# A two-layer diffusion backbone on one NeuronCore: the first adaLN modulation computed with its weights as the stationary operand, group by group

## The reference, cut to what matters

```
mod_x = silu(c) @ w_ada[l] + b_ada[l]          # latent tokens
mod_c = silu(c_ctx) @ w_ada[l] + b_ada[l]      # context tokens
sh1, sc1, g1, sh2, sc2, g2 = split(mod, 6)     # 1024 each
h = rmsnorm(x, g_attn[l]) * (1 + sc1) + sh1    # then h @ w_in[l] and the attention
```

## Time and profile before

| | |
|---|---|
| median of 3 runs | 2082.66 us (2076.31, 2084.02, 2082.66) |
| span of the profiled execution | 2084.2 us |
| PE busy | 1818.6 us, 87% of the span |
| DVE busy | 1218.3 us, 58% |
| ACT busy | 828.5 us, 40% |
| POOL busy | 630.4 us, 30% |
| HBM traffic | 161.48 MB read, 4.19 MB written |

### The profile page before, as it was taken

The page is one execution under the profiler, slowest core; times in us unless marked ns, Lnnn a source line. Parts: engine busy times, 40 slices in busy tenths (PEclk is TensorE's granted clock), DMA queues, the critical chain, the costliest instruction groups (busy, mean ns, idle before and its releaser), DMA issues.

```text
span 2084.2 us, 26369 instructions
## 1 busy us (share of the span) xinstructions
PE 1818.6 (87%) x9456; PEld 1556.0 (75%) x9456; DVE 1218.3 (58%) x2125; ACT 828.5 (40%) x1452; POOL 630.4 (30%) x324
## 2 busy tenths in 40 slices
PE   5877987786896998999999978799886889999997
PEld 1776777674685887888888868778775668888886
DVE  2765757656558688755415665576566466335255
ACT  3345664545423333133213334465555334334242
POOL 1123532212111333422322322252322124444442
PEclk9988999896897999999999989799996889999999
DMA  8210013000142223333324331100100123232332
GB/s 327 85 45 8 1 57 106 20 21 1 61 152 71 99 95 139 123 130 121 101 81 130 122 117 54 38 1 16 51 21 21 51 71 101 93 99 91 101 100 82
DMA packets 45166, 166.94 MB, mean 80 GB/s; under 512 B 4752, under 2 KB 4752, under 8 KB 43920
## 3 DMA queue, kind: packets, MB, share of 16 engines
q1 hardware_dynamic: 41696, 156.25, 22.2%
q10 hardware_dynamic: 3376, 9.44, 1.2%
HBM read 161.48 MB, written 4.19 MB: 79 GB/s over the span
## 4 chain that ended last, share of the span: by engine, by line
PE 67%; DVE 16%; issue 9%; ACT 5%; DMA 2%; DVEq 0%; SPq 0%; POOL 0%; ACTq 0%
PE ps L736 19%; PE ps L737 18%; PE ps L738 18%; DVE nb L1636 2%; PE ps L834 2%; DVE ada_junk L1339 2%; PE ps L835 2%; PE ps L755 2%; PE ps L845 2%; DVE pt_lo L1613 1%; PE ps L933 1%; PE ps L720 1%; ACT qk L1085 1%; DMA w_raw<-w_d 1%; DVE p_sb L1605 1%
## 5 line engine op out<-in xcount | busy, mean ns | idle before, releaser
L667 POOL TENSOR_TENSOR w_lo<-w_raw,w_hi 128x1024 fp32r<-128x1024 f32 (+1 forms) x200 | 474.1, 2374 | 1195.0 <-ACT w_hi L1007 1195.0
L736 PE MATMUL ps<-h_hi,w_hi 128*128 128x512 f32 (+1 forms) x1056 | 376.2, 356 | 5.9 <-DVE h_lo L1427 5.9
L737 PE MATMUL ps<-h_lo,w_hi 128*128 128x512 f32 (+1 forms) x1056 | 376.0, 356 | 0.0
L738 PE MATMUL ps<-h_hi,w_lo 128*128 128x512 f32 (+1 forms) x1056 | 375.2, 355 | 0.0
L1007 ACT ACTIVATE w_hi<-w_raw 128x1024 fp32r<-128x1024 f32 (+1 forms) x200 | 201.3, 1007 | 360.5 <-PE ps L738 236.5
L736 PEld LDWEIGHTS ps<-h_hi,w_hi 128*128 128x128 f32 x1056 | 201.0, 190 | 34.8 <-issue 6.4
L698 POOL TENSOR_TENSOR p_sb<-p_sb,ri 128x768 f32<-128x768 f32 (+1 forms) x120 | 156.1, 1307 | 233.3 <-DVE p_sb L1605 126.6
L737 PEld LDWEIGHTS ps<-h_lo,w_hi 128*128 128x128 f32 x1056 | 201.1, 190 | 28.0
L738 PEld LDWEIGHTS ps<-h_hi,w_lo 128*128 128x128 f32 x1056 | 200.8, 190 | 28.1
L736 PE MATMUL ps<-w_hi,h_hi 128*128 128x384 f32 (+1 forms) x560 | 191.0, 341 | 17.2 <-DVE h_lo L1427 12.4
L1636 DVE TENSOR_REDUCE nb<-ps 128x1 f32<-128x768 f32 (+1 forms) x160 | 135.1, 847 | 111.7 <-PE ps L835 111.4
(11 more groups left out here) (133 smaller groups left out, 3315.4 us busy)
## 6 DMA issues: line engine op xcount, KB each, us to landing
w_raw<-w_d SPq DMA_DIRECT2D x152, 512.0 KB, 3.5
ada_b<-ada_d SPq DMA_DIRECT2D x64, 512.0 KB, 3.6
w_raw<-w_d SPq DMA_DIRECT2D x48, 384.0 KB, 3.1
ada_first<-first_d SPq DMA_DIRECT2D x4, 2048.0 KB, 19.7
ada_first<-ada_d SPq DMA_DIRECT2D x4, 1024.0 KB, 11.5
x_sb<-x_d SPq DMA_DIRECT2D x1, 3072.0 KB, 12.1
x_sb<-x_d ACTq DMA_DIRECT2D x1, 3072.0 KB, 10.3
c_bc<-cc_d SPq DMA_DIRECT2D x2, 1024.0 KB, 8.8
```

The lines of the kernel that those rows point to most:

```text
L667: nc.gpsimd.tensor_tensor(w_lo[:, c % RING, 0:n], w_raw[:, c % RAW, 0:n], w_hi[:, c % RING, 0:n].bitcast(f32), ALU.subtract).then_inc(w_lo ...
L736: nc.tensor.matmul(out, lh, rh, start=first, stop=False)
L737: nc.tensor.matmul(out, lh, rl_, start=False, stop=False)
L738: return nc.tensor.matmul(out, ll, rh, start=False, stop=last)
```

## The change

The stationary and the moving operand change places. For each output feature tile j of a group and each of the eight contraction tiles k, a 128 x 128 block of the weights is the stationary operand and the two columns of silu_cols are the moving one, so that the result stands as feature columns in PSUM at once. `mod_row`, ACT's four copies and PE's sixteen transposes go. The columns of the weights are put in another order in HBM (by the host, as before), so that group g holds scale and shift of the tiles k = 2g and 2g + 1. PE makes groups 0 and 1 ahead of `norm_stats` and groups 2 and 3 behind it. DVE reads groups 0 and 1 before tile k = 0 of the norm, group 2 before k = 2 and group 3 before k = 6. The first projection's matmuls into banks 0 to 3 wait for DVE's read of that group's bank.

```diff
-            def first_modulation():
+            def first_modulation(groups):
-                pe.wait_ge(silu_cols_done, 1)
                 width = FIRST_GROUP * P
-                def columns(g):
-                    pe.wait_ge(mod_row_copied, g + 1)
-                    for c in range(g * FIRST_GROUP, (g + 1) * FIRST_GROUP):
-                        mm = nc.tensor.transpose(ps[:, 4, 2 * c:2 * c + 2], mod_row[:, c * P:(c + 1) * P],
-                                                 ident[0:2, 0:2])
-                    mm.then_inc(first_mod_done, 1)
-                for g in range(FIRST_ADA // FIRST_GROUP):
+                for g in groups:
                     pe.wait_ge(first_ada_loaded[g], 16)
                     w = ada_first[:, g * FIRST_GROUP:(g + 1) * FIRST_GROUP, :].rearrange("p a k -> p (a k)")
-                    for k in range(KT):
-                        mm = nc.tensor.matmul(ps[0:2, g, 0:width], silu_cols[:, k, :],
-                                              w[:, k * width:(k + 1) * width], start=k == 0, stop=k == KT - 1)
-                    mm.then_inc(mod_row_done, 1)
-                    if g:
-                        columns(g - 1)
-                columns(g)
+                    for j in range(FIRST_GROUP):
+                        for k in range(KT):
+                            at0 = k * width + j * P
+                            mm = nc.tensor.matmul(ps[:, g, 2 * j:2 * j + 2], w[:, at0:at0 + P], silu_cols[:, k, :],
+                                                  start=k == 0, stop=k == KT - 1)
+                    mm.then_inc(first_mod_done, 1)
...
                 if l == 0:
+                    pe.wait_ge(silu_cols_done, 1)
+                    first_modulation((0, 1))
                     norm_stats(0)
-                    first_modulation()
+                    first_modulation((2, 3))
...
+                            elif l == 0 and p == 0 and c == 0 and t < FIRST_ADA // FIRST_GROUP:
+                                pe.wait_ge(first_mod_read, t + 1)
...
-                    for g in range(FIRST_ADA // FIRST_GROUP):
-                        act.wait_ge(mod_row_done, g + 1)
-                        width = FIRST_GROUP * P
-                        A(mod_row[:, g * width:(g + 1) * width], ps[0:2, g, 0:width], ACT.Copy) \
-                            .then_inc(mod_row_copied, 1)
...
-            def first_modulation():
-                dve.wait_ge(first_mod_done, FIRST_ADA // FIRST_GROUP)
+            def first_modulation(g):
+                dve.wait_ge(first_mod_done, g + 1)
+                src = ps[:, g, 0:2 * FIRST_GROUP].rearrange("p (k a s) -> p k a s", k=2, a=2)
+                for a, at0 in enumerate((KT + 2 * g, 2 * g)):
+                    for s in range(2):
+                        ins = V.tensor_tensor(mod[:, s, at0:at0 + 2], src[:, :, a, s],
+                                              sm[:, S_BADA + at0:S_BADA + at0 + 2], ALU.add)
+                        if a and s:
+                            ins.then_inc(first_mod_read, 1)
+                        else:
+                            step.mark(ins)
+                step.wait()
+                dve.wait_ge(first_mod_read, g + 1)
                 for s in range(2):
-                    src = ps[:, 4, 0:2 * FIRST_ADA].rearrange("p (c s) -> p c s", s=2)[:, :, s]
-                    step(V.tensor_tensor(mod[:, s, 0:FIRST_ADA], src, sm[:, S_BADA:S_BADA + FIRST_ADA], ALU.add))
-                V.memset(zero[:, :], 0.0).then_inc(ada_used, FIRST_ADA)
-                norm_gains(gs1, KT, S_GATTN)
+                    step.mark(V.scalar_tensor_tensor(gs1[:, s, 2 * g:2 * g + 2], mod[:, s, KT + 2 * g:KT + 2 * g + 2],
+                                                     1.0, sm[:, S_GATTN + 2 * g:S_GATTN + 2 * g + 2],
+                                                     ALU.add, ALU.mult))
+                step.wait()
...
                 if j == 0:
-                    first_modulation()
+                    V.memset(zero[:, :], 0.0).then_inc(ada_used, FIRST_ADA)
...
                 for k in range(KT):
+                    if j == 0:
+                        for g in {0: (0, 1), 2: (2,), 6: (3,)}.get(k, ()):
+                            first_modulation(g)
```

More of the change, by code:

```diff
@@ L330, in backbone @@
     ada_first = place("ada_first", [P, FIRST_ADA, D], f32, R_H)
-    mod_row = place("mod_row", [2, FIRST_ADA * P], f32, R_QKV + 20 * KB)
     ada_b = [place(f"ada_b{i}", [P, D], f32, R_O + (14 + 4 * i) * KB) for i in range(2)]
@@ L413, in backbone @@
         silu_cols_done = sem("silu_cols_done")
-        mod_row_done = sem("mod_row_done")
-        mod_row_copied = sem("mod_row_copied")
+        first_mod_read = sem("first_mod_read")
         first_mod_done = sem("first_mod_done")
@@ L1851 @@
     n_first = FIRST_ADA // FIRST_GROUP
-    first = np.asarray(w_ada)[0][:, :FIRST_ADA * P].reshape(KT, P, n_first, FIRST_GROUP * P)
+    order = [c for k in range(KT) for c in (KT + k, k)]
+    first = np.asarray(w_ada)[0][:, :FIRST_ADA * P].reshape(KT, P, FIRST_ADA, P)[:, :, order, :]
+    first = first.reshape(KT, P, n_first, FIRST_GROUP * P)
     first = np.ascontiguousarray(first.transpose(2, 1, 0, 3).reshape(n_first, P, -1))
```

## The result

The changed kernel takes 2094.28 us (median of 4 runs, 2093.60 to 2096.78) against 2082.39 us (4 runs of before, 2076.31 to 2084.02): ratio 1.0053, interval 1.0037 to 1.0069, so 11.9 us slower by the medians. Run again on another occasion, six runs against eleven, the ratio was 1.0056 (1.0041 to 1.0072).

What follows compares the result with a forecast made beforehand. The first modulation, then DVE's chain to the split at 120.69 us, was taken as the bound. Tile 6 11.4 us later gave 2084.2 + 11.4 = 2095.6 us profiled, 2094.0 us against the median; range 2084 to 2099 us.

Steps and rivals of the forecast that it cites:

- The price of a pass: New modulation's 256 records on PE: 0.213 us each at clock 0.50, 13.65 us for a group.
- Landings and groups: Start of kernel: groups land at 20.7, 25.6, 30.5 and 37.4 us; PE ends group 1 at 48.0 us.
- Statistics: Behind group 1 on PE: 6.45 us as before, to 54.5 us, starting 25.1 us later.
- Rival C: Start of kernel: POOL beside the diagonals and DVE's small readings cost their upper ends, up to +14 us, 2096.5 us; chance 0.07.
- DVE's reading of a group: Before the norm's tiles: four additions and two gains, 1.4 us, bounds 1.0 and 1.8 us.
- DVE's modulation tiles: Behind the norm on DVE's chain to the split: follow by the same 11.4 us.
- Tile 6: Norm on DVE, after waiting for group 3: starts at 83.3 instead of 71.94 us, 11.4 us later.
- PE's wait for the split: In the projection: PE arrives at 128.2 us, split about 132.1 us; wait shrinks from 8.5 to about 4 us.
- The end: Behind 121 us nothing is touched, it only shifts; 2094.0 us against the median.
- Rival A: Modulation: passes raise and hold the clock, 0.112 us each behind 29.46 us; tile 6 10.3 us earlier, 2072.3 us; chance 0.12.
- Rival B: Group 2: spreading of 1/rms lifts the clock for 3.4 us, saving 3.1 us: +8.3 us, 2091.0 us; chance 0.25.

Runs made afterwards that it cites:

- High parts early: Changed kernel with ACT's high parts of units 2 and 3 ahead of the square root, so POOL's splits precede DVE's diagonals: 2093.30 us, ratio 1.0033.
- 128 columns and slow diagonals: Changed kernel with silu_cols repeated to 128 moving columns instead of two, nothing else altered: 2074.21 us, ratio 0.9957.
- quick diagonals: Changed kernel with 128 moving columns and ACT's high parts of units 2 and 3 ahead of the square root: 2067.32 us, ratio 0.9917.

## Why the prediction was right

The forecast was 2094.0 us, the measurement 2094.28 us. By its own steps:

- **The price of a pass**, 0.213 us, which everything hung on: 0.213 and 0.212 us in the changed kernel. That these passes neither raise nor hold the clock was argued from 9.7 us of line 865; the run with all groups behind the statistics shows it over 47.2 us, and 128 moving columns in the same passes undo it.
- **Landings and groups**: group 0 at 20.5 us (forecast 20.7), statistics at 47.84 us (48.0).
- **Statistics**: forecast 6.45 us, measured 8.53 us. This is the term that was mis-sized. I had taken nothing for POOL's splits beside DVE's diagonals, because at 27 us these were paced by PE, with 1.5 us as upper end; they took 4.40 instead of 1.6 us. High parts early took 2.2 us of it back. The measured 2.1 us lies above the upper end of 1.5 us that I had kept. Rival C has an error of its own: its two upper ends, 1.5 us here and 0.4 us for reading group 3, give 13.3 us and not 14 us.
- **DVE's reading of a group**: forecast 1.4 us, measured 84.45 - 83.72 = 0.73 us; four additions pipeline in 0.36 us. That gave back 0.7 us.
- **DVE's modulation tiles**, taken as merely shifted: of the 16 products four take 2.6 us or more, each beside a split of POOL, where three did before, and the last ends 14.8 us late (121.5 instead of 106.7 us).
- **Tile 6**: forecast 83.3 us, measured 84.45 us, so 12.5 instead of 11.4 us late; DVE idle ahead of group 2 for 8.73 (I had said some 11) and ahead of group 3 for 4.40 us (4).
- **PE's wait for the split**: forecast 3.9 us, measured 4.40 us. PE's delay at the start of the projection, 83.54 - 65.84 = 17.7 us, is hidden as far as it exceeds DVE's 13.3 us.
- **The end**: 11.9 us by the medians, less than the 13.3 us at the split. The nearness of the totals to 0.3 us is luck: the statistics were 2.1 us too short and the reading 0.7 us too long, the split came 1.9 us later than forecast, and the part of the shift that is lost behind it hid most of that.

Rival A, the clock raised by the passes, is what 128 columns make of the kernel: forecast for it was tile 6 at 61.6 us and 10.3 us gained; measured 63.31 us, of which 2.8 us are diagonals, and a ratio of 0.9957. The rule that speaks for it in the Trainium skill's page "TensorE: Matmul & The Clock Gate", in "Why this matters for your kernels", that an engine kept busy gets its full clock, did not hold for passes with two moving columns: 0.50 over 47.2 us of gapless records. The same page's section "LDWEIGHTS (loading the stationary operand)" gives a load one price, its columns divided by 1.2 GHz, and no second one for the other level of the clock; here the same load came every 0.11 us at 1.00 and every 0.21 us at 0.50. Rival B occurred in the run with all groups behind the statistics, as a stretch of 3.4 us, and saved there about the 3.1 us that were forecast for it: 256 passes took 51.51 us, where 256 x 0.212 us are 54.3 us. Neither profile of the changed kernel holds a level before 86 us, but the spacing of 0.212 us over groups 2 and 3 leaves no room for it there.

Not settled: why the shift, 13.3 us at the split, is 11.3 us at the feed-forward of layer 0 and 7.5 us at the end of one profile, 9.4 and 8.0 us in the other. Part of it is PE itself. PE busy behind the split, before and then in the changed kernel:

```profile
121.00:2084.00 1963.00, 1737.26 (x9100) 0.93 0.22 73
134.30:2091.00 1956.70, 1733.67 (x9100) 0.93 0.22 74
```

The same 9100 records keep PE busy for 3.6 us less in the changed kernel's profile. The levels of the clock lie at other places in each execution, which would fit, but no run isolated them, and part of it is only that the profiled execution before was a slow one of its kind.

## What to carry to other kernels

Before the operands of a matrix-vector product are swapped to get rid of transposes, price the pass at both levels of the clock: in these runs TensorE dropped to half speed with one or two moving columns and stayed there, however busy it looked. Repeating the moving columns by a stride of zero up to the width of the stationary operand cost nothing here, 0.11 us a pass at 1.00 of the clock with 2 or 128 columns, and gave the clock back. And when statistics are moved, look at what has moved beside them: beside the two splits on POOL six small operations of DVE took 4.4 instead of 1.6 us, in the middle of the path.

## What was not expected of the hardware

- 128 moving float32 columns under a 128 x 128 float32 load cost no more than two: 0.11 us a pass at 1.00 of the clock, 0.21 us at 0.50. The 512 columns of the old form took 0.43 us at 1.00, so 128 of them are about 0.11 us by that, an estimate, as much as the load; together they still took 0.11 us, so load and columns ran beside each other.
- DVE's 128 x 128 diagonals beside POOL's float32 splits: 4.40 us for six instead of 0.87 us for four and 0.71 us for two, because two of them took up to 1.85 us instead of 0.28 us. The slowdown by 2.8 us exceeds what the one modulation tile beside such a split had shown (1.5 us).
- Short waits of PE in the middle of such a chain can cost twice: with 128 columns and slow diagonals PE waited 0.90, 1.22 and 0.97 us for them, and the clock was at 0.50 from 41.3 to 48.1 us; with quick diagonals PE waited 0.90 us once, and the clock didn't fall before 103.7 us.
